# Second weights ahead of silu in the late-norm FFNs, conditioning by pairs in the prologue, the memory's norm moved into the fourth FFN

## The reference, cut to what matters

```python
# first block, per layer l
mod = silu(c) @ ada_w[l] + ada_b[l]        # 1024 x 9216: the conditioning, 36 units of 256 columns
h = rmsnorm(x, ffn1_norm[l]) * (1 + sc1) + sh1
x = x + 0.5 * gt1 * swiglu(h, ffn1_w_in[l], ffn1_w_out[l])
x = x + gt2 * mixed(...)                   # attention, convolution, gated linear attention
h = rmsnorm(x, ffn2_norm[l]) * (1 + sc3) + sh3
x = x + 0.5 * gt3 * swiglu(h, ffn2_w_in[l], ffn2_w_out[l])
# second block
mem_n = rmsnorm(mem, norm_mem)             # 256 x 1024, first used after the first block
for i in range(4):
    x = x + mixer_i(rmsnorm(x, norm_mix[i]))
    x = x + cross_attention(rmsnorm(x, norm_cross[i]), mem_n, ...)
    x = x + swiglu(rmsnorm(x, norm_ffn[i]), ffn_w_gu[i], ffn_w_down[i])
out = rmsnorm(x, norm_final)
```

## Time and profile before

| what | value |
|---|---|
| median of 3 runs | 2744.11 us (2741.28 to 2746.25) |
| the profiled execution | 2737.76 us |
| its span | 2736.0 us |
| TensorE busy in the span | 2664.8 us (97%) |
| VectorE busy | 1858.1 us (68%) |
| ScalarE busy | 1352.1 us (49%) |
| HBM read | 529.68 MB, 195 GB/s over the span |
| TensorE's mean granted clock | 0.989 of full |

### The profile page before, as it was taken

How to read it: one execution, slowest core, us unless ns; L and a number is a source line. 1 busy time by engine, 2 the same in 40 slices (tenths; PEclk the granted TensorE clock), 3 DMA queues, 4 the chain that set the end, 5 groups by cost and what they waited for, 6 DMA issues and landing times.

```text
span 2736.0 us, 52868 instructions
## 1 busy us (share of the span) xinstructions
PE 2664.8 (97%) x22247; PEld 2598.4 (95%) x22247; DVE 1858.1 (68%) x2525; ACT 1352.1 (49%) x1616; POOL 3.5 (0%) x7
## 2 busy tenths in 40 slices
PE   6999999999999999999999999999999999999998
PEld 5899889999998899999999989999999999999998
DVE  6888967878889555676555775565665655765654
ACT  4334654444456644565544536544555444655443
POOL 0000000000000000000000000000000000000000
PEclk7899999999999999999999999999999999999999
DMA  6998528979974265745365634355664456643553
GB/s 221 326 297 281 192 86 285 289 256 297 303 257 143 83 209 192 238 139 170 110 212 185 207 118 143 109 197 199 200 200 140 157 201 211 197 148 119 179 192 106
DMA packets 457928, 533.06 MB, mean 195 GB/s; under 512 B 9895, under 2 KB 434081, under 8 KB 457633
## 3 DMA queue, kind: packets, MB, share of 16 engines
q1 hardware_dynamic: 456468, 530.12, 59.2%
q10 hardware_dynamic: 1293, 0.65, 0.1%
HBM read 529.68 MB, written 2.63 MB: 195 GB/s over the span
## 4 chain that ended last, share of the span: by engine, by line
PE 88%; DVE 5%; DMA 3%; issue 2%; ACT 1%; SPq 1%; DVEq 0%; ACTq 0%
PE ps L2289 14%; PE ps L2112 13%; PE ps L2113 13%; PE ps L2114 13%; PE ps L2132 9%; PE ps L2793 6%; DMA work<-in_ada_w 3%; DVE work L1392 2%; PE ps L2585 2%; PE ps L2587 2%; PE ps L2586 2%; PE ps L2478 2%; PE ps L2323 2%; PE ps L2763 1%; PE ps L2745 1%
## 5 line engine op out<-in xcount | busy, mean ns | idle before, releaser
L1288 DVE TENSOR_TENSOR wlo<-raw,whi 128x2048 fp32r<-128x2048 f32 (+1 forms) x514 | 976.2, 1918 | 380.4 <-ACT whi L795 380.1
L795 ACT ACTIVATE whi<-raw 128x2048 fp32r<-128x2048 f32 (+1 forms) x514 | 827.5, 1616 | 414.6 <-PE ps L2114 172.1
L2112 PE MATMUL ps<-hhi,whi 128*128 128x256 f32 x1824 | 516.2, 283 | 3.6 <-DVE wlo L1288 2.2
L2113 PE MATMUL ps<-hlo,whi 128*128 128x256 f32 x1824 | 506.5, 278 | 0.0
L2114 PE MATMUL ps<-hhi,wlo 128*128 128x256 f32 x1824 | 505.9, 277 | 0.0
L2112 PE MATMUL ps<-parts_f,whi 128*128 128x256 f32 x1344 | 372.6, 277 | 7.8 <-issue 7.8
L2113 PE MATMUL ps<-parts_f,whi 128*128 128x256 f32 x1344 | 371.6, 276 | 0.0
L2114 PE MATMUL ps<-parts_f,wlo 128*128 128x256 f32 x1344 | 371.2, 276 | 0.0
L2289 PE MATMUL ps<-ghi,whi 128*128 128x256 f32 x1280 | 355.4, 278 | 6.4 <-DVE wlo L1288 6.3
L2112 PEld LDWEIGHTS ps<-hhi,whi 128*128 128x128 f32 x1824 | 344.4, 189 | 13.2 <-issue 13.0
L2289 PE MATMUL ps<-glo,whi 128*128 128x256 f32 x1280 | 355.2, 278 | 0.0
(11 more groups left out here) (302 smaller groups left out, 4558.5 us busy)
## 6 DMA issues: line engine op xcount, KB each, us to landing
raw<-in_ffn_w_in SPq DMA_DIRECT2D x88, 1024.0 KB, 10.5
raw<-in_ffn_w_gu SPq DMA_DIRECT2D x88, 1024.0 KB, 5.1
work<-in_ada_w SPq DMA_DIRECT2D x72, 1024.0 KB, 8.9
raw<-in_ffn_w_out SPq DMA_DIRECT2D x88, 512.0 KB, 6.0
raw<-in_ffn_w_down SPq DMA_DIRECT2D x88, 512.0 KB, 5.5
raw<-in_ca_w_kv SPq DMA_DIRECT2D x32, 1024.0 KB, 5.5
raw<-in_mix_w_in SPq DMA_DIRECT2D x24, 1024.0 KB, 5.5
raw<-in_da_w_in SPq DMA_DIRECT2D x24, 1024.0 KB, 5.8
```

Of the source, the lines that this page charges most:

```text
L795: f(whi[:, s, 0:size], raw[:, s, 0:size], ACT.Copy).then_inc(hi_done[s], 1)
L1288: tt(wlo[:, s, 0:size], raw[:, s, 0:size], whi[:, s, 0:size].bitcast(F32), ALU.subtract).then_inc(lo_done[s], 1)
L2112: mm(dst, wh, xh, start=first, stop=False)
L2113: mm(dst, wh, xl, start=False, stop=False)
```

## The change

Six things change.

- In the late-norm FFNs, at step 0, ACT rounds A(1) ahead of silu of step 0, and B(1) ahead of the rounding of the product.
- The memory leaves the prologue. ACT issues its load at the end of the second mixer of the first block. PE transposes three quarters of it right after the sum of the norm ahead of the fourth FFN, the last quarter behind step 0, and sums the squares behind step 3. ACT copies, squares, takes the root and rounds in steps 0, 1, 2, 5 and 7; DVE adds, scales and subtracts in steps 3, 6 and 8. Steps 2 and 3 of that FFN leave PE's loop and are written out.
- In the prologue all eight units go by pairs on DVE; `ada_direct` is gone.
- The constants and first rows are issued by ACT, and SP begins with units 0 to 3. Units 8 to 11 and the first O0 are sent already in the prologue. SP waits for the relative-bias line between O0 and O1 of step 0.
- The bias line and the lambda sums move on DVE from the prologue to behind the product of step 0 of the first FFN. B(0) of the first FFN is rounded ahead of the norm's own roundings.
- The sine and cosine arguments are spread over steps 2 to 8 of the first FFN, and ACT's two sine instructions go from step 8 to step 9.

The diff, cut to its core:

```diff
@@ tiles
-        tok_mem, tok_x = (raw[:, n, :].rearrange("p (t d) -> p t d", t=ST) for n in range(2))
-        mem = raw[:, 2, :].rearrange("p (k s) -> p k s", k=KT)
+        tok_x = raw[:, 1, :].rearrange("p (t d) -> p t d", t=ST)
+        tok_mem, mem = work(8192, ST, D), work(10240, KT, S)
+        MEM_BANKS = (5, 7, 3, [st for st in stages if st.kind == "ffn"][3].slots[2])
@@ SP
-                    load(q["mem_in"], tok_mem, a["mem_2"].rearrange("o (t p) d -> p (o t) d", p=P))
...
                     load(q["token_in"], tok_x, a["x"].rearrange("o (t p) d -> p (o t) d", p=P))
-                    for u in range(4, 6):
-                        ada(u)
-                    stream(1)
-                    for u in range(6, 8):
+                    for u in range(4, 8):
                         ada(u)
                     stream(2)
+                    for u in range(8, 10):
+                        ada(u)
+                    stream(3)
+                    for u in range(10, 12):
+                        ada(u)
+                    stream(5)
                     sp.wait_ge(*PRO.at(0, "line"))
                     load(q["line_out"], line, bias_line[0:8, :])
@@ ACT, norm
-                if i == 1:
+                if st.mod == (0, 0):
                     ahead(-1, 1)
...
+                if st.mod == (0, 0):
+                    ahead(-1, 2)
@@ ACT, ffn
                     ahead(pa)
                     if st.defer is not None:
+                        if j == 0:
+                            ahead(pb, 1)
                         act.wait_ge(read[A], st.reads[A] + j + 1)
                         f(silu_a, silu_a, ACT.Silu).then_inc(q["ffn_silu"], 1)
...
                     ahead(pb)
                     if j:
                         ahead(o1, AHEAD if j < STEPS - 1 else 2)
+                    elif st.defer is not None:
+                        ahead(pb + 1, 1)
...
+                    if (st.i, j) == (3, 0):
+                        mem_tiles(0)
+                        mem_tiles(1)
...
+                    if (st.i, j) == (3, 7):
+                        mem_high()
@@ ACT, end of the mixer
+                if l == 1:
+                    act.wait_ge(q["gla_lo"], 2)
+                    nc.scalar.dma_start(tok_mem, a["mem_2"].rearrange("o (t p) d -> p (o t) d", p=P))\
+                        .then_inc(q["mem_in"], 16)
@@ DVE
             def prologue(st):
                 first_columns(st)
                 ada_pair(2, 1)
+                ada_pair(4, 0)
                 other_columns(st)
-                bias_and_lambda()
...
+                    if (st.i, j) == (0, 0):
+                        bias_and_lambda()
@@ PE
+                for p in range(4):
+                    turn_tiles(tok_x, p, 4 + p).then_inc(q["tok_turned"], 1)
+                ada_pair(0, 0, 3)
+                ada_pair(2, 1, 3)
...
-                for u in range(*ADA_BY_PE):
-                    ada_direct(u, 3)
...
+                if st.mod == (0, 0):
+                    late_rows()
+                    ada_pair(4, 0, 3)
...
+                    ada_pair(6, 1, 3)
+                if st.mod == (1, 2):
+                    for p in range(3):
+                        mem_turn(p)
...
+                    if first and st.i == 3:
+                        pe.wait_ge(q["mem_copied"], 2)
...
+                    if st.i == 3 and n == 0:
+                        mem_turn(3)
+                    if st.i == 3 and n == 3:
+                        mem_sum()
```

More of the change, by code:

```diff
@@ L447, in build @@
         stages.append(Stage(kind="prologue"))
-        norm("norm_mem_2", 0, [(q["tok_copied"], p + 1) for p in range(4)], 2, source="mem")
         stages.append(Stage(kind="start"))
-        ready = [(q["tok_copied"], p + 5) for p in range(4)]
+        ready = [(q["tok_copied"], p + 1) for p in range(4)]
         for l in range(DEPTH1):
@@ L733, in _ @@
                         for j in range(STEPS - 1):
-                            stream(st.pos + 2 + 4 * min(j + 1, STEPS - 1))
-                            for n in range(per[j]):
+                            stream(st.pos + 2 + 4 * (j + 1))
+                            for n in range(per[j] if st.i or j else 0):
                                 ada(u + n)
@@ L802, in load @@
                     nc.scalar.dma_start(dst, src).then_inc(semaphore, 16)
+                load(q["const_in"], con[:, 0:N_FIRST], a["constants"][:, 0:N_FIRST])
+                for name in FIRST_ROWS:
+                    load_row(load, q["rows_first"], name)
                 later = [name for name in ROWS if name not in FIRST_ROWS]
-                for name in later[:8]:
+                for name in later[:4]:
                     load_row(load, q["rows_in"], name)
@@ L808, in prologue @@
                 f(silu_c[:, :], col("c", 0, KT), ACT.Silu).then_inc(q["c_ready"], 1)
-                for name in later[8:]:
+                for name in later[4:]:
                     load_row(load, q["rows_in"], name)
@@ L817, in prologue, with mem_tiles, mem_squares, mem_root @@
                          a[name].partition_broadcast(P).rearrange("p a b -> p (a b)"))
-                for p in range(4):
-                    act.wait_ge(q["tok_turned"], p + 1)
-                    f(mem[:, 2 * p:2 * p + 2, :], ps[:, 4 + p, :], ACT.Copy).then_inc(q["tok_copied"], 1)
+            def mem_tiles(p):
+                act.wait_ge(q["mem_turned"], p + 1)
+                f(mem[:, 2 * p:2 * p + 2, :], ps[:, MEM_BANKS[p], :], ACT.Copy).then_inc(q["mem_copied"], 1)
+            def mem_squares(p):
+                act.wait_ge(q["mem_copied"], p + 1)
+                f(norm_x[:, 2 * p:2 * p + 2, :], mem[:, 2 * p:2 * p + 2, :], ACT.Square).then_inc(q["mem_sq"], 1)
+            def mem_root():
+                log_exp_tables()
+                act.wait_ge(q["mem_ss"], 1)
+                f(rstd[:, 0, :], ps[:, MEM_BANKS[3], 0:S], ACT.Ln, bias=eps, scale=1.0 / D).then_inc(q["mem_ln"], 1)
+                act.wait_ge(q["mem_ln"], 1)
+                f(rstd[:, 1, :], rstd[:, 0, :], ACT.Exp, scale=-0.5).then_inc(q["mem_rs"], 1)
+            def mem_high():
+                for k in range(KT):
+                    act.wait_ge(q["mem_t"], k + 1)
+                    f(mhi[:, k, :], mem[:, k, :], ACT.Copy).then_inc(q["mem_hi"], 1)
             def rope_tables():
@@ L1341, in turned_angle, with less_turns @@
                 pro(name + "_c", ts(turns, turns, magic, None, ALU.subtract))
+            def less_turns(name, dst):
                 pro(name + "_d", stt(dst, turns, -t1, angle, ALU.mult, ALU.add))
@@ L1344, in turned_angle, with bounded @@
                 pro(name + "_f", stt(dst, turns, -t3, dst, ALU.mult, ALU.add))
+            def bounded(name, dst, shift):
                 if shift:
@@ L1347, in turned_angle, with mem_added, mem_scaled, mem_low @@
                 pro(name, ts(dst, dst, 3.1415925, -3.1415925, ALU.min, ALU.max))
+            def mem_added():
+                for p in range(1, 4):
+                    dve.wait_ge(q["mem_sq"], p + 1)
+                    if p > 1:
+                        dve.wait_ge(q["mem_add"], p - 1)
+                    tt(norm_x[:, 0:2, :], norm_x[:, 0:2, :], norm_x[:, 2 * p:2 * p + 2, :], ALU.add)\
+                        .then_inc(q["mem_add"], 1)
+            def mem_scaled():
+                dve.wait_ge(q["mem_rs"], 1)
+                for k in range(KT):
+                    stt(mem[:, k, :], mem[:, k, :], col("norm_mem_2", k), rstd[:, 1, :], ALU.mult, ALU.mult)\
+                        .then_inc(q["mem_t"], 1)
+            def mem_low():
+                for k in range(KT):
+                    dve.wait_ge(q["mem_hi"], k + 1)
+                    tt(mlo[:, k, :], mem[:, k, :], mhi[:, k, :].bitcast(F32), ALU.subtract).then_inc(q["mem_lo"], 1)
             def lambdas():
@@ L1464, in norm @@
                 low(KT - 1)
-                if i:
-                    ahead(st.pos)
+                ahead(st.pos)
             def ffn(st):
@@ L2304, in ffn @@
                 u0, per = st.ada or (0, 10 * (0,))
-                for n in range(2):
+                apart = 4 if st.i == 3 else 2
+                for n in range(apart):
                     step(n, n == 0)
```

152 lines of the change are left out of this document (82 added, 70 removed).

## The result

| | before | after |
|---|---|---|
| median | 2742.9 us (2741.28 to 2746.25, 4 runs) | 2720.31 us (2719.93 to 2725.02, 4 runs) |
| profiled execution | 2737.76 us | 2720.22 us |

The ratio is 0.992, with a 95% interval of 0.9907 to 0.9932: 0.8% faster, clear of the noise, and inside the range that was given. The profiled executions differ by 17.5 us (forecast 16.4), the medians by 22.6.

What follows compares the result with a forecast made beforehand. Bounds: loads waiting for buffers and PE's slow small work in the prologue, mainly DVE in the first FFN, PE behind 263 us. 9.1 + 1.2 + 1.2 + 7.3 - 2.4 = 16.4 gives 2721.4 profiled, 2727.7 us median; range 2718 to 2738.

Steps and rivals of the forecast that it cites:

- Prologue: Start to the first FFN's first product: that product at 46.5 us instead of 55.64, a gain of 9.1 us.
- follow x without a hole: +6.0: Prologue: units 4 and 5 land 6.0 us after x, at 27.5 to 29.5 us, their buffers being free in time.
- The rule on issuing engines: Prologue: all issuers share 16 DMA engines, so ACT issuing small loads saves only issue time, at most 2.1 us.
- First FFN with sine and cosine: First FFN: 1.2 us from B(0) rounded earlier and units 8 to 11 already there, 1.2 from spreading the arguments.
- Late-norm FFNs: Last four FFNs: earlier A(1) and B(1) rounding removes eight PE waits of 7.8 us, less 0.5: gain 7.3 us.
- Fourth FFN: Taking on the memory's work costs 2.4 us: 1.4 on PE behind step 0, 1.0 for two ACT copies; the rest hidden.
- the rival in which this FFN pays for all: Fourth FFN: ACT and DVE delays reach PE, 34 us if all exposed, outweighing the other terms' 18.8; slower, 4%.
- before's distance of 6.35 us from profile to median: Whole kernel: the median lies 6.35 us above the profiled execution, added to 2721.4 to predict 2727.7 us.
- rivals on the late-norm waits: Last four FFNs: PE waits at B(1) what it saved at A(1); gain without the 7.3, so 2735 us; 8%.
- on the prologue (first product at 52): Prologue stays bound by the conditioning: gain there 3.6 us instead of 9.1, total gain 10.9, time 2733 us; 14%.
- The last rival: First FFN: PE's waits at 88 to 116 us shrink and the clock holds, 8.6 us at stake; 2725 or less; 12%.

Runs made afterwards that it cites:

- free places: Changed kernel with conditioning units 4 and 5 landing in the still empty places of O0 and A(0), sent without waiting for the first pair: median 2720.5 us.
- later broadcasts: Changed kernel with positions and four lambda vectors (384 KB) issued by ACT behind the first norm's squares: median 2722.26 us, 0.9925 against before.
- the second: Changed kernel with units 4 and 5 in O0's and A(0)'s empty places and the 384 KB of broadcasts issued later: median 2718.43 us, 0.9916 against before.

## Why the prediction was right, step by step

The range and the direction were right, and the sum was right on the profiled executions: 16.4 us forecast, 17.5 measured. Its terms were not all right for the reasons that were given.

- **Prologue, 9.1 forecast, 8.46 measured.** The path was named rightly: landing of units 4 and 5, third pair, copies, fourth pair, A(0)'s rest. Two steps on it were off in opposite directions, and that they cancelled was luck. Unit 3 and x landed at 16.8 and 19.6, 2 to 4 us earlier than forecast. I then let units 4 and 5 "follow x without a hole: +6.0"; they needed 10.2. SP's wait for the first pair does leave a hole of 1.5 us in the first parts, but filling it moved the third pair by nothing; moving the broadcasts brought 1.0 us, with the hole or without. The other 3 us are the lag of the last part, whose cause stays open. Of the 8.46 us, the memory's MiB is 2.4 by experiment; the 1.65 us of earlier issue are 0.24. The remaining 5.8 I lay, by the traces, on DVE having taken over from PE the direct units and on the freed order; that was not run by itself.
- **The rule on issuing engines.** I had weighed against the second issuing engine that all issuers share the same 16 engines (the Trainium skill, "DMA: Bandwidth & Descriptors", section "Issuing engines are not separate DMA queues"). The trace agrees: issued by ACT beside SP's large loads, the small ones let PE's first transpose start at 8.40 us, issued by SP ahead of them at 3.94. And of the issue time that was saved, 1.65 us, only 0.24 reached the first product and nothing the median.
- **First FFN with sine and cosine, 2.4 forecast, 2.05 measured against the profiled execution.** The size came out, the mechanism did not: that is luck. I had counted on less waiting. The idle time ahead of the second two pairs is gone as forecast, but the next pair waits 5.03 us, which I had not listed, and PE's idle time in this FFN is 12.2 us against 11.8. The gain is 2.6 us less of PE's busy time, at a clock of 0.97 against 0.95. Two other traces with the old code of this FFN have 222.34 and 222.07 us from first product to root; against these the changed kernel is 7.0 and 6.7 us shorter, and all ten traces with the new code lie under 216.5. So against an ordinary execution of before this term was too small by more than 4 us. What it is made of (B(0) rounded first, the early units 8 to 11, the spread arguments) was not run apart, except for the last.
- **Late-norm FFNs, 7.3 forecast, 9.5 measured** three times over. The mechanism held; the term was mis-sized by reading the waits' sum as their cost (1.3 us hidden by the records, 0.6 by the slow first matmul behind each wait) and by taking 0.5 off for a margin that was not needed.
- **Fourth FFN, 2.4 forecast, 1.36 measured on the profiled executions.** Its profile of before had 3.4 us at half clock behind the norm's gap; the second trace of before had a clock of 1.00 there and took 190.12 us. Against that one the cost is 2.3, and by parts: 1.0 for the two copies (the wait at B(1) of 1.21 us was forecast as about 1.3), 1.3 for the transposes behind step 0 and the sums of squares (forecast 1.4). So the term was right, and the 1.36 is too low by chance. No wait in steps 1 to 8: the rival in which this FFN pays for all is excluded. Two slips in that rival change nothing: half of its 34 us does not yet outweigh 18.8, and two thirds of it give 2748, not 2749.
- **The median.** I carried before's distance of 6.35 us from profile to median over to the changed kernel. There the profile lies on the median. That is the error left in 2727.7 against 2720.31: 1.1 us from the sum, 6.3 from the carried distance. The traces show where before's slower executions lose: one of three had its first product at 60.77 instead of 55.64 and 55.84, and two of three took 5 us more in the first FFN. For the first, PE's chain of direct units and squares set the first product, and it is longer when the clock falls earlier. Now DVE sets it: in five traces of the same prologue or nearly so the long stretch at half clock began between 35.1 and 38.4 us, and the first product stood at 46.97 to 47.58. For the second, why the waits of the first FFN no longer grow is not shown. So part of the 22.6 us was not in the sum at all.

The rivals on the late-norm waits (no gain) and on the prologue (first product at 52) are excluded by the segments and the row at 47.18. The last rival expected less waiting of PE at 88 to 116 and a clock that holds, with 2725 us or less. The median lies there, and the clock did hold better (0.91 against 0.85 over that stretch), but the waits hardly shrank: 6.2 us in three (82 to 103 us now) against 6.5 in three.

## What to carry to other kernels

Price a term from segments between fixed points of two traces where you can; a sum of recorded waits of PE is too small, here by 0.16 us a wait that the record overlaps and 0.07 that the first matmul behind it loses. Take the same points on both sides: a norm's root is a bad cut where what stands between it and the first product has changed. Where two engines race (pairs on DVE against the rests that PE needs), take a second profile of the old kernel before adding its distance to the median: one trace can be 5 us from the next with the same code. And when a wait is for a load, look when its last part lands, not when it was issued: sending units 6 us earlier won nothing.

## What the hardware showed that was not expected

The 16 parts of a 1-MiB load land within 0.4 to 1.2 us of each other up to 19.6 us of the changed kernel's program (with free places and later broadcasts too) and within 3 to 4 us afterwards. For unit 6 with 384 KB of broadcasts beside it the spread was 5.4 and 6.5 us (27.5 to 34.0 in the second). Meanwhile DMA as a whole moved 328 to 352 GB/s with free places (18 to 30 us). The lag stays as long as load follows load and is gone (0.5 to 0.6 us) behind a pause of the queue. In the kernel before it is there too, 2.3 to 2.7 us from unit 2 on. And PE's granted clock stood at half from 34 us on in one execution and fell there only between 38 and 40 in another with the same code of the prologue: 5 us at the first product.
